# A transformer block on one core: weights of the gated branch stage split three granules ahead from one column block earlier

## What is computed

```
h   = rmsnorm(x) ; z = h @ w_in + b_in          # q, k, v, gates of both branches, gm, gf
y_m = mLSTM branch(z), y_f = forgetting attention(z)          # 512 wide each
mix = sigmoid(gm) * (y_m @ w_br_mlstm) + sigmoid(gf) * (y_f @ w_br_fox)
x   = x + mix @ w_out
x   = x + (silu(h2 @ w_gate) * (h2 @ w_up)) @ w_down,  h2 = rmsnorm(x)
out = rmsnorm(x)
```

## Time and profile before

| | |
|---|---|
| time, median of 3 runs | 761.53 us (761.28 to 761.6) |
| the profiled execution, its time | 761.63 us |
| its span | 759.9 us |
| PE busy | 747.3 us, 98% of the span |
| DVE busy | 529.3 us, 70% |
| ACT busy | 312.4 us, 41% |
| mean granted TensorE clock | 0.997 |

### The profile page before, as it was taken

The page is one execution under the profiler, slowest core; times in us unless marked ns, Lnnn a source line. Parts: engine busy times, 40 slices in busy tenths (PEclk is TensorE's granted clock), DMA queues, the critical chain, the costliest instruction groups (busy, mean ns, idle before and its releaser), DMA issues.

```text
span 759.9 us, 11767 instructions
## 1 busy us (share of the span) xinstructions
PE 747.3 (98%) x4755; PEld 655.7 (86%) x4755; DVE 529.3 (70%) x806; ACT 312.4 (41%) x492; POOL 24.1 (3%) x51
## 2 busy tenths in 40 slices
PE   8999999999999999999999999999999999999996
PEld 7988888888676788899888999999999998888885
DVE  5878734347988587986356799999999998533123
ACT  5553213344555343443335344444444445433111
POOL 4000000011200000000000000000000000000000
PEclk9999999999999999999999999999999999999999
DMA  8533323301111031516511313333332334321302
GB/s 244 146 111 111 111 67 127 111 1 56 57 57 57 15 97 56 166 57 212 201 59 56 111 56 112 111 113 111 105 86 93 106 112 166 111 100 66 111 0 111
DMA packets 61802, 75.25 MB, mean 99 GB/s; under 512 B 3682, under 2 KB 49842, under 8 KB 61748
## 3 DMA queue, kind: packets, MB, share of 16 engines
q1 hardware_dynamic: 61744, 74.50, 30.5%
q10 hardware_dynamic: 4, 0.00, 0.0%
HBM read 72.40 MB, written 2.10 MB: 98 GB/s over the span
## 4 chain that ended last, share of the span: by engine, by line
PE 69%; DVE 2%; issue 1%; ACT 1%; POOLq 0%; POOL 0%; ACTq 0%; DVEq 0%
PE bank L1546 22%; PE bank L1548 21%; PE bank L1547 21%; PE bank L1809 1%; PE bank L1771 1%; PE bank L1792 1%; DVE w_lo L943 1%; ACT w_hi L584 0%; DVE t_lo L1323 0%; PE bank L1778 0%; PE bank L1559 0%; DVE t_sum L1319 0%; PE bank L1775 0%; DVE mix_sum L1393 0%; DVE mix_sum L1388 0%
## 5 line engine op out<-in xcount | busy, mean ns | idle before, releaser
L943 DVE TENSOR_TENSOR w_lo<-stage,w_hi 128x1024 fp32r<-128x1024 f32 (+1 forms) x125 | 139.1, 1122 | 114.3 <-ACT w_hi L584 105.3
L1546 PE MATMUL bank<-hT_hi,w_hi 128*128 128x256 f32 (+1 forms) x588 | 193.9, 330 | 0.7 <-issue 0.4
L1548 PE MATMUL bank<-hT_hi,w_lo 128*128 128x256 f32 (+1 forms) x588 | 191.2, 325 | 0.0
L1547 PE MATMUL bank<-hT_lo,w_hi 128*128 128x256 f32 (+1 forms) x588 | 191.1, 325 | 0.0
L584 ACT ACTIVATE w_hi<-stage 128x1024 fp32r<-128x1024 f32 x126 | 122.9, 977 | 143.1 <-PE bank L1548 134.5
L1546 PEld LDWEIGHTS bank<-hT_hi,w_hi 128*128 128x128 f32 x588 | 111.9, 190 | 9.9 <-issue 1.1
L1548 PEld LDWEIGHTS bank<-hT_hi,w_lo 128*128 128x128 f32 x588 | 111.8, 190 | 9.3
L1547 PEld LDWEIGHTS bank<-hT_lo,w_hi 128*128 128x128 f32 x588 | 111.9, 190 | 8.2
L1546 PE MATMUL bank<-t_hi,w_hi 128*128 128x256 f32 x368 | 104.4, 284 | 2.0 <-DVE w_lo L943 2.0
L1547 PE MATMUL bank<-t_lo,w_hi 128*128 128x256 f32 x368 | 104.1, 283 | 0.0
L1548 PE MATMUL bank<-t_hi,w_lo 128*128 128x256 f32 x368 | 104.1, 283 | 0.0
(11 more groups left out here) (218 smaller groups left out, 1052.4 us busy)
## 6 DMA issues: line engine op xcount, KB each, us to landing
stage<-in_w_in SPq DMA_DIRECT2D x21, 1024.0 KB, 5.2
stage<-in_w_gate SPq DMA_DIRECT2D x11, 1024.0 KB, 5.3
stage<-in_w_up SPq DMA_DIRECT2D x11, 1024.0 KB, 5.3
stage<-in_w_down SPq DMA_DIRECT2D x22, 512.0 KB, 4.5
stage<-in_w_out SPq DMA_DIRECT2D x4, 1024.0 KB, 8.9
x_nat<-in_x SPq DMA_DIRECT2D x4, 512.0 KB, 5.7
stage<-in_w_br_mlstm SPq DMA_DIRECT2D x4, 512.0 KB, 3.4
stage<-in_w_br_fox SPq DMA_DIRECT2D x4, 512.0 KB, 4.5
```

The source lines that it names most:

```text
L943: dve.tensor_tensor(ring_part(w_lo, g), staged(g), ring_part(w_hi, g).bitcast(F32), ALU.subtract).then_inc(lo_split, 1)
L1546: pe.matmul(o, a_hi, b_hi, start=first, stop=False)
L1547: pe.matmul(o, a_hi, b_lo, start=False, stop=False)
L1548: return pe.matmul(o, a_lo, b_hi, start=False, stop=last)
```

## The change

`br_ahead` changes from "two ahead" to "three ahead" two granules earlier: at the first branch granule of block 1 (39) and no longer at the first gate granule of block 2 (41).

```
-            if g < br_first[2]:
+            if g < br_first[2] - 2:
                 return [g + AHEAD]
-            return [a for a in ([g + AHEAD] if g == br_first[2] else []) + [g + AHEAD + 1] if a < G_OUT + AHEAD]
+            return [a for a in ([g + AHEAD] if g == br_first[2] - 2 else []) + [g + AHEAD + 1] if a < G_OUT + AHEAD]
```

## The result

| | before | after |
|---|---|---|
| median | 761.6 us (761.28 to 761.94, 9 executions) | 763.31 us (763.05 to 764.83, 9 executions) |
| profiled execution: time, span | 761.63, 759.9 us | 763.19, 761.5 us |
| ratio after to before | | 1.0027, 95% interval 1.0017 to 1.0037 |

The change makes the kernel 0.27% slower, 1.7 us by the medians. The forecast was 761.8 us with a range to 762.8; the nine executions all lie above the range. What happened is rival B, the fall of the clock, which the prediction had put at 763.5.

The account below looks back on a forecast made before the run. The prediction took DVE's backlog up to run sum 1 to set PE's restart at granule 45. DVE's 0.19 us of extra idle time gave 761.63 + 0.19 = 761.8 us, range 761.0 to 762.8.

Parts of the forecast that it names:

- rival B: The single pause of 3.3 us ahead of granule 45 drops TensorE's clock to half: 763.5 us, chance 0.10.
- What bounds the stage: PE's restart at granule 45 is set by DVE's whole backlog, up to run sum 1; PE loses 3.1 us there.
- the label "issue": The profile's name for PE's 0.4 us pause ahead of granule 45; the prediction said it waits for run sums.
- DVE's and ACT's new times: Low part of granule 42 starts at 293.96, that of 43 at 299.95; run sum 1 ends at 310.01.
- The rows of the next block: Profile rows one block later, already in the new order, used as pattern: 6.16 us from `mixT_lo` to run sum 1's end.
- Three pauses become one of 3.1: PE's pauses at granules 42, 43 and 45 become one ahead of 45, about 3.26 us; restart 0.19 later.
- the clock still stands at 1.00 when granule 45 begins: After the single long pause PE resumes at the full 2.4 GHz; chance 0.10 that it does not.
- The reason given for the 0.10: At the kernel's end a pause of 4 us, 754 to 758, left the clock at 1.00; chance of a fall 0.10.
- rows 7: Profile rows of the clock: a fall after patchy work at 7 to 8, half speed 3.4 us; 1.00 at the end.
- The price of rival B: 3.4 us at half speed from granule 45's restart, in which PE does 1.7 us less work: 761.8 + 1.7 = 763.5 us.
- Rivals A and C: Pause before granule 45 is issue, gone: -3.1, 758.6 us, chance 0.06; full ring blocks earlier splits: 761.6 us, within forecast's 0.84.

Follow-up runs that it names:

- sums_first: Changed kernel, with run sums 0 and 1 in the first run made ahead of granule 45's split and weight sums; 760.58 us, ratio to before 0.9986.
- pause_filled: Changed kernel, with 24 superfluous matmuls on PE in the pause ahead of granule 45; 761.85 us, ratio to before 0.9999.
- only_43: Changed kernel, but only granule 43's split moves (42 and 43 both at 40); 761.78 to 761.89 or 762.96 to 764.72 us; run again, 763.26.
- after_again: The changed kernel run once more, unaltered, to look inside one execution; 764.58 us.
- first eight experiments: Follow-up kernels of the first two comparisons, four each; the kernel before ran beside them, medians 761.72 us (33 executions) and 761.55 us (22).
- before_again: The kernel before the change run once more, unaltered, to look inside one execution; 762.57 us.
- only_42_again: Changed kernel with only granule 42's split moved ahead, 43's left where it was, run a second time for a trace; 762.13 us.

## Why the prediction was wrong

- **What bounds the stage** held. PE's restart at granule 45 waits for run sum 1, the label "issue" notwithstanding: the changed kernel's own trace names line 1299, and moving the run sums (`sums_first`) removed the wait.
- **DVE's and ACT's new times** held: 293.96, 299.95 and 310.01 were measured as 294.05, 300.04 and 310.10, with the stage 0.09 later. The rows of the next block were a good pattern for the new order, down to the idle 0.45 (0.44).
- **Three pauses become one of 3.1**: held (3.12), with the 0.19 it costs; `pause_filled` has the forecast time, 761.85.
- **The step that failed is that the clock still stands at 1.00 when granule 45 begins.** The sum has no term for the clock, its fall was left to rival B with a chance of 0.10, and the range ended at 762.8 without it. The runs showed the clock falling with the one long pause in each of the ten executions of the changed kernel (by their times; two are traced), for 1.28 us in the profiled one.
- **The reason given for the 0.10** is the end of the trace, where PE does nothing from 754 to 758 with the clock at 1.00. The shown rows stop half a microsecond short of the fall. The next stretch of the same trace is the first line here; the second is the end of `only_43`, whose last matmul ends at 754.22:

```profile
758.00:759.90 1.90, 0.00 (x0) 0.00 (x0) 0.00 (x0) 0.00 (x0) 0.00 (x0) 0.63 0.54 204
756.00:758.00 2.00, 0.00 (x0) 0.00 (x0) 0.48 (x1) 0.72 (x1) 0.51 (x1) 0.56 0.05 19
```

  So in the kernel before the clock fell at about 758.5, 4.5 us after PE's last matmul had ended (753.96), and in `only_43` at about 756.2, 2.0 us after it. Over the ends of all 14 traces this time spreads from 2.0 to 5.3 us (worked out from the mean clock of stretches of one microsecond; no matmul runs there by whose duration the clock could be verified). One draw of such a spread says nothing of a pause of 3.1 us: in the changed kernel the clock fell 2.6 us after the last matmul (307.08 to 309.66). The other half of rows 7, the fall after patchy work at 7 to 8, was the better guide.
- **The price of rival B** was 1.7 us, oversized, and its time of 763.5 came out in part by luck. It took matmuls at half speed to be twice as far apart; they are 0.21 us apart in place of 0.12, so that a slow stretch of 3.4 us, fully paid, costs 1.5 (`only_43_again`), and in the profiled execution 0.5 us of it fell into the pause, which leaves 1.28. Other executions of the changed kernel paid more, up to 2.7 (`after_again`).
- **The Trainium skill's rule** that I set against the change ("TensorE: Matmul & The Clock Gate", section "Why this matters for your kernels", that long pauses between bursts of matmuls send the clock back to half) agrees with the traces of the changed kernel, where the clock fell in a pause of 3.12 us. The time that it gave by rival B, 763.5, is 0.2 from the median. The runs add that in some executions the clock fell with single pauses down to 1.73 us.
- **Rivals A and C** fell. PE did not go on at 306.9, and the splits came as early as the change says.
- **The kernel before wasn't at its floor either.** Its pause of 1.72 let the clock fall in some executions, by their times 13 of the 55 that ran beside the first eight experiments (one such execution is traced, `before_again`); none of the nine first ones showed it.

## What to carry to other kernels

When PE waits on a chain of work on another engine, splitting inputs earlier only moves the wait to the next thing that the chain has to deliver; find the last item that PE needs from the chain and move that one forward, or let PE ask for it later. Several short pauses added together aren't the same as one long one: the sum here rose by 0.2 us, and the clock took 1.3 more in one traced execution and 2.7 in the other. A stretch in which the clock stayed up once is no proof that a shorter pause is safe; look for the same stretch in other executions. If a pause can't be removed, superfluous matmuls in it are cheap insurance, here 1.5 us. And where the times of a kernel fall into groups, look at each group's clock before comparing medians.

## What the runs showed of the hardware

By their times, TensorE's granted clock fell with a bracket of 3.12 in all ten executions of the changed kernel (two of them traced); with 2.57 in eight of twelve (one traced), with 1.93 in eight of twelve (one traced), with 1.73 in 13 of 55; eleven executions each with 1.63, with 1.45 and without any bracket show no second group of times. These counts come from comparisons on different chips, and the kernel before alone had none of nine, ten of 33 and three of 22, so they give no safe length of a pause. The fall came at different moments: 2.4 to 2.6 us into the pause, or 0.4, 1.0 and 1.2 us behind its end (`only_43_again`, `before_again`, `only_42_again`); at the end of the kernel, 2.0 to 5.3 us after the last matmul. At half speed the 256-column matmuls start 0.21 us apart in place of 0.12, not twice as far. The slow stretch lasted 3.4 us in four of the profiled falls and 6.8 in the fifth, with no pause to prolong it.

The record of the clock isn't complete. In the trace of the changed kernel, at the kernel's start, PE's timeline has

```profile
12.13 0.41 PE L1547 MATMUL bank<-hT_lo,w_hi 128*128 128x256 f32 x1
12.34 0.41 PE L1548 MATMUL bank<-hT_hi,w_lo 128*128 128x256 f32 x1
```

and its stretches give a clock of 1.00 for the same time:

```profile
12.00:13.00 1.00, 1.00 (x7) 1.00 (x8) 1.00 (x2) 1.00 (x2) 0.78 (x1) 1.00 1.23 259
```

Matmuls of 0.41 are those of half speed, so the record misses a slow stretch here. Read the durations beside the clock; an execution's mean clock, which depends on what was recorded at its start and end too, tells little.
